# Moving part of the values' compression from a batch's end into the next batch, and its last product behind the dilated values

## The chip, the cores and the metric

The kernel runs on one core of a Trainium2 chip. The metric is the device time of one execution in microseconds. Its engines are PE (TensorE, matrix products; its weight loads are PEld), DVE (VectorE), ACT (ScalarE), POOL (GpSimd) and SP (SyncE, which here only issues DMAs). Each engine works its instructions off in program order; semaphores order them against each other.

## The reference

One inference step of a decoder with two layers, for a prompt of 512 rows and for eight sample sequences ("batches") of eight new rows with 2048 past positions. All is float32. Each layer norms and projects its rows, runs two groups of attention heads, and ends with an output projection and a squared-ReLU MLP. What matters here is the sparse group on the samples:

```python
# per batch: raw cached K/V rows -> 127 compressed tokens per K/V and head
parts.append(einsum('bncskd,scdh->bnskh', chunk + pe_half, w1[:, half]))   # 16 positions a chunk, 2 halves
hid = silu(sum(parts))
kvc = einsum('bnskh,shd->bnskd', hid, w2)          # s = 0 keys, s = 1 values
p_cmp = softmax(q . kvc_keys - alibi)
o_cmp = p_cmp . kvc_values
top   = 16 blocks of 64 rows by the summed p_cmp ("choice")
o_sel = attention over the chosen blocks (selection cache)
o_win = attention over the last 512 rows
```

The other group is an attention over dilated rows (distances 1, 4 and 16). The new rows' keys take part in each ("new scores").

## The kernel before

A layer is worked off in four stages: the projections (`project`), the prompt's attention in four rounds of twelve steps (`prompt_steps`), eight sample batches (`batch`, seven of them in a hardware loop with `more` true, the last one behind it), and 36 units of the output projection and the MLP (`unit`). The change touches the third and its two borders.

Nothing is scheduled by a planner: the order of each engine is the order of the text, and the same batch runs on all five engines at once. `Count.at(i, k)` is the value that a semaphore has after the k-th event of iteration i.

**PE in a batch**, `batch(it, more)` from L1357: the dilated scores of classes 0, 1 and 2 (L1371, 72 instructions in one row of a timeline), the new dilated rows (L1388); the second product of the compressed keys (L1395) and of the compressed values (L1401) from `hid`; the scores of the compressed, window and new keys (L1408 to L1413); the last dilated class (L1371 again), for which `kda` is loaded a second time by ACT (L758); importance sums and a transpose (L1421, L1425); the selection scores in two halves (L1431), of which the second goes into the bank that DVE reads importance from (L1994); transposes of the window's (L1441) and the dilated probabilities (L1449); the dilated values (L1463 to L1465, with one small product L1457 between); compressed and window values into bank 6 (L1470 to L1473); the transposes of the selection (L1480 to L1484); the selected values (L1496, L1500); the gathering of the outputs into bank 6 (L1508, L1513). Between the last of these stand the first products of the compression of the *next* batch, `compress(s, lo, hi, at)` (L1297): step j of 16 multiplies `w1[:, s, j]` with both heads' raw rows of residue j % 8 (two products, which the trace shows as four instructions); s is 0 for keys and 1 for values; the result gathers in a PSUM bank. After its last step, `h_full` is signalled. All 21 steps at the end of the batch are one group of 84 instructions in line L1303.

**The raw rows** lie in `raw`, one half of `ring` (2 MB), for one batch at a time. SP (from L524) reads the page numbers of batch b + 1 (L475), waits until both of batch b's hidden products are full (`h_full` at 2, L527), and only then issues nine of its sixteen raw pages; it waits for the dilated scores, issues the dilated keys (L496, L497), the other seven raw pages, waits for the window's and the dilated values' products, issues the window (L493) and the dilated values (L500), waits for the selected values' product and issues the sixteen selected pages (L478 stands for raw and selected pages alike). PE waits for all sixteen raw pages before the first key step of the next batch (L1487).

**The hidden layer** between the two products is made by ACT (`hidden_exp`, L744) and DVE (`hidden_batch`, L1930 to L1942: add one, reciprocal, multiply), one after the other for s = 0 and 1 at the end of a batch, through one buffer `he`. DVE then copies the compressed keys (L1971) and values (L1972), makes biased scores, the choice (L1993 to L2002), the minimum over the selection scores (L2017, L2020), and the outputs (L2026, L2033, L2054).

In a layer's first batch the raw rows were loaded beside the prompt, and `prompt_steps` holds 24 of the 32 steps of the compression at m = 12, 13 and 14, four ahead of and four behind the last products of the prompt (L1320 to L1335); L1520 has the other eight.

## Time and profile before

| | |
|---|---|
| median of three runs | 2443.39 us (2442.29 to 2445.78) |
| profiled execution | 2435.86 us, of which 2434.0 are its span |
| PE busy | 2291.6 us (94% of the span) |
| DVE, POOL, ACT busy | 904.7, 646.0, 553.0 us |
| mean share of the DMA engines, q1 | 47.0% |
| chain that ended last | PE 84%, DVE 5%, issue 5%, DMA 3%, ACT 2% |
| L1303 (compression) | 2048 instructions, 9% of the chain |

Busy time says which engine works, not what it waits for; the chain of waits says, backwards from the end, what each step was released by. A line L1303 is line 1303 of the kernel. In a timeline each row has a start, a duration, an engine, a line, the operand names and a count of merged instructions; brackets at its end are idle time ahead of it and who ended it. An averaged share hides that the stages differ: the sample batches run from about 384 to 709 us and from 1582 to 1905 us of the span.

### The profile page before, as it was taken

The numbers are of one execution on the slowest core, as the hardware profiler recorded it, in microseconds if no ns is written. First come the engines' busy times: TensorE is split into PE (matmuls) and PEld (weight loads), VectorE is DVE, ScalarE is ACT, GpSimd is POOL, SyncE is SP. The second block draws the span as 40 slices with busy tenths as digits, with TensorE's granted clock in tenths as the row PEclk, the third lists the DMA queues.
The fourth block names the chain that finished last, engine by engine and source line by source line (L and its number), as shares of the span: only waits on it lengthen the run. The fifth ranks groups of instructions, "written<-read, shape, count | busy, mean of one in ns | idle before, by whom it ended". The sixth has DMA issues, their size and how long they took to land.

```text
span 2434.0 us, 43176 instructions
## 1 busy us (share of the span) xinstructions
PE 2291.6 (94%) x13534; PEld 1610.0 (66%) x13534; DVE 904.7 (37%) x2423; ACT 553.0 (23%) x1306; POOL 646.0 (27%) x719
## 2 busy tenths in 40 slices
PE   7999888898899999999999998889899999999998
PEld 4544556667666777777745455667667667777776
DVE  2002663434344232336510146443433532223374
ACT  2101651111112422120211036411111133222202
POOL 0000771000132343434100037510010524343441
PEclk9999999999999999999999999999999999999999
DMA  9542016777863454445365220277777644454441
GB/s 342 197 166 74 23 53 242 247 284 261 298 238 149 165 209 175 176 162 200 122 259 190 104 86 0 79 280 289 257 287 259 241 159 163 163 211 173 178 161 40
DMA packets 128529, 448.19 MB, mean 184 GB/s; under 512 B 17921, under 2 KB 89474, under 8 KB 107266
## 3 DMA queue, kind: packets, MB, share of 16 engines
q1 hardware_dynamic: 118768, 416.45, 47.0%
q10 hardware_dynamic: 9618, 29.98, 3.6%
q8 instruction: 71, 1.16, 0.2%
q14 instruction: 72, 0.59, 0.1%
HBM read 435.76 MB, written 152.57 MB: 242 GB/s over the span
## 4 chain that ended last, share of the span: by engine, by line
PE 84%; DVE 5%; issue 5%; DMA 3%; ACT 2%; DVEq 1%; ACTq 0%; SPq 0%; POOLq 0%
PE bank L1036 37%; PE bank L1119 16%; PE bank L1303 9%; PE bank L1463 3%; DMA zone<-in_dilated_k 2%; PE bank L1250 2%; PE bank L1238 2%; PE bank L1371 2%; PE bank L1270 2%; PE bank L1496 1%; ACT zone L682 1%; PE bank L1017 1%; PE bank L1135 1%; PE bank L1465 1%; PE bank L1480 1%
## 5 line engine op out<-in xcount | busy, mean ns | idle before, releaser
L1036 PE MATMUL bank<-zone,ring 128*128 128x288 f32 x1664 | 425.8, 408 | 7.8 <-DVE zone L1637 5.2
L1119 PE MATMUL bank<-ring,hT 128*128 128x512 f32 (+3 forms) x960 | 396.4, 566 | 6.5 <-ACTq L727 5.0
L1036 PEld LDWEIGHTS bank<-zone,ring 128*128 128x128 f32 x1664 | 315.6, 190 | 101.3 <-DVE zone L1637 10.7
L1036 PE MATMUL bank<-zone,w 128*128 128x288 f32 x1408 | 353.6, 406 | 0.0
L1036 PEld LDWEIGHTS bank<-zone,w 128*128 128x128 f32 x1408 | 267.5, 190 | 73.9
L1119 PEld LDWEIGHTS bank<-ring,hT 128*128 128x128 f32 (+1 forms) x960 | 168.9, 181 | 197.3 <-issue 183.1
L1303 PE MATMUL bank<-ring,w 128*128 128x128 f32 x2048 | 242.4, 277 | 0.0
L845 POOL TENSOR_TENSOR w<-ring 128x512 f32<-128x512 f32 x72 | 94.8, 1317 | 553.3 <-PE bank L1036 312.3
L1303 PEld LDWEIGHTS bank<-ring,w 128*128 128x128 f32 x2048 | 233.1, 192 | 3.8 <-issue 3.8
L956 POOL TENSOR_TENSOR zone<-constants,stat 128x1024 f32<-128x1024 f32 x16 | 30.4, 1897 | 522.8 <-DVE stat L2002 522.8
L607 ACT COPY zone<-bank 128x288 f32<-128x288 f32 x72 | 28.7, 398 | 563.4 <-PE bank L1036 563.4
L1036 PE MATMUL bank<-xT,ring 128*128 128x288 f32 x512 | 136.0, 409 | 2.0 <-ACT zone L607 2.0
L682 ACT ACTIVATE zone<-zone,stat 128x128 f32<-128x128 f32 (+1 forms) x192 | 106.2, 554 | 102.9 <-DVE stat L1779 102.9
L1036 PEld LDWEIGHTS bank<-xT,ring 128*128 128x128 f32 x512 | 97.2, 191 | 29.6 <-ACT zone L607 2.9
L848 POOL TENSOR_TENSOR w<-w,ring 128x512 f32<-128x512 f32 x72 | 109.5, 1522 | 13.4 <-POOL w L845 13.4
L1779 DVE CUSTOM_DVE_ANT_0 zone<-bank,zone 128x128 f32<-128x128 f32 (+1 forms) x192 | 86.4, 488 | 71.7 <-PE bank L1238 63.9
L874 POOL COPY zone<-zone 128x128 f32<-128x128 f32 (+1 forms) x24 | 9.7, 403 | 361.5 <-ACT zone L654 361.5
L599 ACT ACTIVATE ring<-ring,gains 128x256 f32<-128x256 f32 x256 | 105.3, 494 | 0.0
L852 POOL TENSOR_TENSOR w<-ring,w 128x512 f32<-128x512 f32 x72 | 99.8, 1386 | 12.8 <-POOL ring L849 11.1
L1250 PE MATMUL bank<-c_ident,zone 128*128 128x128 f32 x480 | 75.6, 282 | 25.9 <-ACT zone L692 23.6
L1250 PEld LDWEIGHTS bank<-c_ident,zone 128*128 128x128 f32 x480 | 51.8, 142 | 69.9 <-issue 67.6
L654 ACT ACTIVATE zone<-bank,stat 128x512 f32<-128x512 f32 (+3 forms) x50 | 32.4, 648 | 284.8 <-PE bank L1119 284.8
(250 smaller groups left out, 2818.1 us busy)
## 6 DMA issues: line engine op xcount, KB each, us to landing
out_dil_s<-in_state_kv_dil SPq DMA_DIRECT2D x48, 2720.0 KB, 12.2
ring<-in_w_units SPq DMA_DIRECT2D x72, 1024.0 KB, 4.8
zone<-in_dilated_v SPq DMA_DIRECT2D x16, 3072.0 KB, 10.6
ring<-in_cache_kv_cmp SPq DMA_DIRECT2D x256, 128.0 KB, 2.6
ring<-in_cache_kv_sel SPq DMA_DIRECT2D x256, 128.0 KB, 5.7
ring<-in_w_in SPq DMA_DIRECT2D x10, 2048.0 KB, 8.0
zone<-in_dilated_k SPq DMA_DIRECT2D x16, 1280.0 KB, 5.9
zone<-in_dilated_k SPq DMA_DIRECT2D x16, 1024.0 KB, 7.8
```

Of the source, the lines that this page charges most:

```text
L599: last = nc.scalar.activation(w_[:, h, k], w_[:, h, k], ACT.Copy, scale=gain_of(l * 2 + 1, 4 * h + k))
L682: nc.scalar.activation(p_sb[:, slot, k, 0:w], p_sb[:, slot, k, 0:w], ACT.Exp, scale=-1.0, bias=stat[:, 16 + at:17 + at], accum_out=stat[:, ...
L845: nc.gpsimd.tensor_tensor(c_[:, 0], w_[:, 2], w_[:, 3], ALU.add).then_inc(s_comb.sem, 1)
L848: nc.gpsimd.tensor_tensor(c_[:, 1], c_[:, 0], w_[:, 0], ALU.subtract).then_inc(s_comb.sem, 1)
L852: nc.gpsimd.tensor_tensor(c_[:, 2], w_[:, 1], c_[:, 1], ALU.subtract).then_inc(s_comb.sem, 1)
L1036: last = mm(dst[:, 0:HALF], lhs[:, k, :], rhs(k), start=first and k == 0, stop=(k == 3), skip_group_check=True)
L1119: last = mm(dst, hT[:, k, t * P:t * P + ROWS[t]], ring[:, n % 2, k * CH:k * CH + width], start=start and k == 0, stop=stop and k == KT - 1)
L1238: last = mm(bank[2 * (m % 2) + k][:, 0:w], q[rows, t * P:(t + 1) * P], kT[rows, 0:w], start=True, stop=True)
L1250: last = tr(bank[4 + k][:, c * P:(c + 1) * P], p_sb[:, slot, k, c * P:(c + 1) * P], ident[:])
L1303: last = mm(out[:, k, first:first + P], w1[:, s, j, :], rawt[:, :, s, k, j % 8, :], start=(j == 0 and k == 0), stop=(j == 15 and k == 1), ...
L1463: mm(bank[7][32 * g:32 * g + M, :], ptd[:, e, at:at + M], vd[:, j, :], start=(j == 0), stop=False, skip_group_check=True)
L1779: V.tensor_tensor_reduce(p_sb[:, slot, k, 0:w], bank[2 * (m % 2) + k][:, 0:w], (p_bias if m < STEPS_A else p_biasd)[:, k, SEQ - w:SEQ], -1 ...
```

## The change

Of the values' 16 steps of compression, the first six (`V_AHEAD`) stay at the end of the batch in front; four (up to `V_NEW`) come behind the new scores and six (up to `V_CHOICE`) behind the choice's last transpose, both within the batch that uses them. They gather in bank 6 (`VHID_BANK`) in place of bank 5, behind a wait until DVE has taken the last outputs out of it. The second product of the values and DVE's copy of it move behind the dilated values, and the compressed values' product behind the window's. `hidden_exp` and `hidden_batch` are called once for the keys at the end of a batch and once for the values within it: on ACT behind the dilated probabilities, on DVE behind the minimum. In a layer's first batch, three and three value steps stand in the prompt's last step in place of four and four, and the eight behind it go. SP's program is not changed.

```diff
@@ -80,11 +80,12 @@
 TD_SD, TD_PTC, TD_PTW, TD_PTD, TD_PTS, TD_N = 0, 1, 2, 3, 4, 6
-SC_KTC, SC_VC, SC_S, SC_WIN, SC_NEW, SC_IMP, SC_SEL, SC_LEAST, SC_SUM, SC_OUT, SC_N = (
-    0, 1, 2, 3, 4, 5, 6, 8, 9, 10, 11)
+SC_KTC, SC_S, SC_WIN, SC_NEW, SC_IMP, SC_SEL, SC_LEAST, SC_VC, SC_SUM, SC_OUT, SC_N = (
+    0, 1, 2, 3, 4, 5, 7, 8, 9, 10, 11)
 SC_BANK = {SC_KTC: 2, SC_VC: 3, SC_S: 4, SC_WIN: 5, SC_NEW: 2, SC_IMP: 3, SC_SEL: 2, SC_SEL + 1: 3,
            SC_LEAST: 2, SC_SUM: 2, SC_OUT: 6}
-HID_BANK, FIRST_HID = (4, 5), (2, 3)
+HID_BANK, FIRST_HID, VHID_BANK = 4, 2, 6
+V_AHEAD, V_NEW, V_CHOICE, V_SEL = 6, 10, 16, 16
...
@@ -736,15 +737,15 @@
-                def hidden_exp(it, at):
-                    for s in range(2):
-                        act.wait_ge(h_full.sem, h_full.at(it, s + 1))
-                        act.wait_ge(h_done.sem, h_done.at(it, s))
-                        nc.scalar.activation(
-                            he.rearrange("p (k n) -> p k n", k=2),
-                            bank[at[s]][:, 0:258].rearrange("p (k n) -> p k n", k=2)[:, :, 1:129],
-                            ACT.Exp, scale=-1.0, bias=ncbias[:, s:s + 1]).then_inc(s_hexp.sem, 1)
+                def hidden_exp(it, s, at):
+                    act.wait_ge(h_full.sem, h_full.at(it, s + 1))
+                    act.wait_ge(h_done.sem, h_done.at(it, s))
+                    act.sem_inc(waits_taken_act, 1)
+                    nc.scalar.activation(
+                        he.rearrange("p (k n) -> p k n", k=2),
+                        bank[at][:, 0:258].rearrange("p (k n) -> p k n", k=2)[:, :, 1:129],
+                        ACT.Exp, scale=-1.0, bias=ncbias[:, s:s + 1]).then_inc(s_hexp.sem, 1)
@@ -763,6 +764,7 @@
                     probs(s_d, 3, slice(0, P))
+                    hidden_exp(it, 1, VHID_BANK)
                     act.wait_ge(td_full.sem, td_full.at(it, TD_PTW + 1))
...
-                hidden_exp(l * NB, FIRST_HID)
+                hidden_exp(l * NB, 0, FIRST_HID)
                 with act.Fori(0, NB - 1) as b:
                     batch(b)
-                    hidden_exp(l * NB + b + 1, HID_BANK)
+                    hidden_exp(l * NB + b + 1, 0, HID_BANK)
                 batch(NB - 1)
@@ -1318,21 +1320,23 @@
-                        compress(0, 0, 4, FIRST_HID[0])
+                        compress(0, 0, 4, FIRST_HID)
...
                     if ends and m == STEPS + 2:
-                        compress(1, 0, 4, FIRST_HID[1])
+                        pe.wait_ge(og_a.sem, og_a.at(l, ROUNDS))
+                        pe.sem_inc(waits_taken_pe, 1)
+                        compress(1, 0, V_AHEAD // 2, VHID_BANK)
...
                     if ends and m == STEPS + 2:
-                        compress(1, 4, 8, FIRST_HID[1])
+                        compress(1, V_AHEAD // 2, V_AHEAD, VHID_BANK)
@@ -1395,12 +1399,6 @@
-                    pe.wait_ge(h_done.sem, h_done.at(it, 2))
-                    B = bank[SC_BANK[SC_VC]]
-                    for k in range(2):
-                        last = mm(B[:, k * HD:(k + 1) * HD], hid[:, 1, k * P:(k + 1) * P], w2[:, 1, :],
-                                  start=(k == 0), stop=(k == 1), skip_group_check=True)
-                    last.then_inc(sc_full.sem, 1)
@@ -1412,6 +1410,7 @@
                     mm(B[low, 64:128], q_a, kns[:], start=True, stop=True, skip_group_check=True).then_inc(
                         sc_full.sem, 1)
+                    compress(1, V_AHEAD, V_NEW, VHID_BANK)
                     pe.wait_ge(kda_ld.sem, kda_ld.at(it, 2))
                     dilated_class(ND_A + 4).then_inc(td_full.sem, 1)
@@ -1423,6 +1422,7 @@
                     tr(bank[TD_PTC % 2][:, 0:64], s_c, ident[0:64, 0:64]).then_inc(td_full.sem, 1)
+                    compress(1, V_NEW, V_CHOICE, VHID_BANK)
                     pe.wait_ge(sel_ld.sem, sel_ld.at(it, NPG))
@@ -1465,13 +1465,20 @@
-                    pe.wait_ge(sc_used.sem, sc_used.at(it, 0))
+                    pe.wait_ge(sc_used.sem, sc_used.at(it, SC_LEAST + 1))
+                    pe.wait_ge(h_done.sem, h_done.at(it, 2))
+                    B = bank[SC_BANK[SC_VC]]
+                    for k in range(2):
+                        last = mm(B[:, k * HD:(k + 1) * HD], hid[:, 1, k * P:(k + 1) * P], w2[:, 1, :],
+                                  start=(k == 0), stop=(k == 1), skip_group_check=True)
+                    last.then_inc(sc_full.sem, 1)
                     O = bank[6][:, 0:P]
-                    mm(O[low], ptc, vc, start=True, stop=True, skip_group_check=True)
                     for c in range(4):
                         mm(O[high], ptw[:, c, :], kw_sb[:, c, 128:256], start=(c == 0), stop=False, skip_group_check=True)
-                    mm(O[high], ptw[0:64, 4, :], vsm[:, 128:256], start=False, stop=True,
-                        skip_group_check=True).then_inc(win_pv.sem, 1)
+                    mm(O[high], ptw[0:64, 4, :], vsm[:, 128:256], start=False, stop=True, skip_group_check=True)
+                    pe.wait_ge(sc_used.sem, sc_used.at(it, SC_VC + 1))
+                    pe.sem_inc(waits_taken_pe, 1)
+                    mm(O[low], ptc, vc, start=True, stop=True, skip_group_check=True).then_inc(win_pv.sem, 1)
...
@@ -1514,10 +1521,11 @@
                     if more:
-                        compress(0, 11, 16, HID_BANK[0])
-                        compress(1, 0, 16, HID_BANK[1])
-                compress(1, 8, 16, FIRST_HID[1])
+                        compress(0, 11, 16, HID_BANK)
+                        pe.wait_ge(sc_used.sem, sc_used.at(it, SC_OUT + 1))
+                        pe.sem_inc(waits_taken_pe, 1)
+                        compress(1, 0, V_AHEAD, VHID_BANK)
@@ -1927,20 +1935,20 @@
-                def hidden_batch(it, at):
-                    horder = Order(ch_h, it)
-                    for s in range(2):
-                        dve.wait_ge(s_hexp.sem, s_hexp.at(it, s + 1))
-                        V.tensor_scalar(he, he, 1.0, None, ALU.add).then_inc(horder.sem, 1)
-                        dve.wait_ge(horder.sem, horder.next())
-                        V.reciprocal(he, he).then_inc(horder.sem, 1)
-                        dve.wait_ge(horder.sem, horder.next())
-                        V.scalar_tensor_tensor(
-                            hid[:, s, :].rearrange("p (k n) -> p k n", k=2),
-                            bank[at[s]][:, 0:258].rearrange("p (k n) -> p k n", k=2)[:, :, 1:129], cbias[:, s:s + 1],
-                            he.rearrange("p (k n) -> p k n", k=2), ALU.add, ALU.mult).then_inc(h_done.sem, 1)
-                    if horder.k != 4:
+                def hidden_batch(it, s, at):
+                    horder = Order(ch_h, it, 2 * s)
+                    dve.wait_ge(s_hexp.sem, s_hexp.at(it, s + 1))
+                    dve.sem_inc(waits_taken_dve, 1)
+                    V.tensor_scalar(he, he, 1.0, None, ALU.add).then_inc(horder.sem, 1)
+                    dve.wait_ge(horder.sem, horder.next())
+                    V.reciprocal(he, he).then_inc(horder.sem, 1)
+                    dve.wait_ge(horder.sem, horder.next())
+                    V.scalar_tensor_tensor(
+                        hid[:, s, :].rearrange("p (k n) -> p k n", k=2),
+                        bank[at][:, 0:258].rearrange("p (k n) -> p k n", k=2)[:, :, 1:129], cbias[:, s:s + 1],
+                        he.rearrange("p (k n) -> p k n", k=2), ALU.add, ALU.mult).then_inc(h_done.sem, 1)
+                    if horder.k != 2:
                         raise ValueError(horder.k)
...
@@ -1969,7 +1977,6 @@
                     V.tensor_copy(ktc, small(SC_KTC)[:, 0:P]).then_inc(sc_used.sem, 1)
-                    V.tensor_copy(vc, small(SC_VC)[:, 0:P]).then_inc(sc_used.sem, 1)
                     negated(s_c, small(SC_S)[low, 0:P], const["b_cmp"][:], stat[low, 24:25]).then_inc(sc_used.sem, 1)
@@ -2020,6 +2027,7 @@
                     V.tensor_tensor(stat[:, 27:28], small(SC_LEAST)[:, 0:1], sm[:, 19:20], ALU.min).then_inc(sc_used.sem, 1)
                     dve.wait_ge(sc_used.sem, sc_used.at(it, SC_LEAST + 1))
                     dve.sem_inc(s_max.sem, 1)
+                    hidden_batch(it, 1, VHID_BANK)
...
+                    V.tensor_copy(vc, small(SC_VC)[:, 0:P]).then_inc(sc_used.sem, 1)
                     dve.wait_ge(od_full.sem, od_full.at(it, 1))
...
-                hidden_batch(l * NB, FIRST_HID)
+                hidden_batch(l * NB, 0, FIRST_HID)
                 with dve.Fori(0, NB - 1) as b:
                     batch(b)
-                    hidden_batch(l * NB + b + 1, HID_BANK)
+                    hidden_batch(l * NB + b + 1, 0, HID_BANK)
                 batch(NB - 1)
```

## Rows read from the trace of the kernel before

**Rows 1.** Chain that ended last, whole span: start, duration, engine, line, count.

```profile
455.19 1.90 PE bank L1496 x32
...
498.98 1.90 PE bank L1496 x32
...
540.12 1.90 PE bank L1496 x32
...
705.73 1.94 PE bank L1496 x32
...
1878.14 2.78 PE bank L1371 x72
...
1900.94 1.94 PE bank L1496 x32
```

**Rows 2.** Timeline of PE, one batch of layer 0: start, duration; idle before in brackets.

```profile
547.24 9.62 PE L1303 MATMUL bank<-ring,w 128*128 128x128 f32 x84
556.70 2.94 PE L1371 MATMUL bank<-zone 128*128 128x128 f32 x72
...
560.98 0.66 PE L1401 MATMUL bank<-w,zone 128*128 128x64 f32 x4
561.56 0.32 PE L1408 MATMUL bank<-zone,q_s 128*64 128x128 f32 x1
...
563.96 1.08 PE L1371 MATMUL bank<-zone 128*32 128x128 f32 x32 [1.20 <-DMA zone<-in_dilated_k]
...
567.59 1.08 PE L1431 MATMUL bank<-ring,q_s 128*64 128x512 f32 x4 [1.07 <-DVE topk L1994]
...
570.07 0.66 PE L1449 MATMUL bank<-c_ident,zone 128*128 128x128 f32 x4 [0.95 <-DVE zone L2006]
571.53 2.08 PE L1463 MATMUL bank<-zone 128*128 128x512 f32 x10 [0.81 <-ACT zone L773]
...
578.23 1.09 PE L1480 MATMUL bank<-c_ident,zone 128*128 128x128 f32 x8
...
579.67 1.58 PE L1303 MATMUL bank<-ring,w 128*128 128x128 f32 x12
```

**Rows 3.** Timeline of SP's queue, the same batch.

```profile
561.61 5.30 SPq L478 DMA_DIRECT2D ring<-in_cache_kv_cmp  x9
...
568.33 3.92 SPq L478 DMA_DIRECT2D ring<-in_cache_kv_cmp  x7
...
583.68 7.77 SPq L478 DMA_DIRECT2D ring<-in_cache_kv_sel  x16
```

**Rows 4.** Timeline of PE, the start of each layer's first batch.

```profile
384.46 2.17 PE L1371 MATMUL bank<-zone 128*128 128x128 f32 x40 [2.84 <-DMA zone<-in_dilated_k]
...
1582.34 1.84 PE L1371 MATMUL bank<-zone 128*128 128x128 f32 x28 [2.73 <-DMA zone<-in_dilated_k]
```

**Rows 5.** Timeline of DVE, the batch of rows 2.

```profile
550.67 1.75 DVE L1937 RECIPROCAL zone<-zone 128x256 f32<-128x256 f32 x1
...
574.18 0.16 DVE L2020 TENSOR_TENSOR stat<-bank,sm 128x1 f32<-128x1 f32 x1 [0.47 <-PE bank L1457]
```

**Rows 6.** Line L475 on SP, from 590 to 603 us.

```profile
L475 SPq TENSOR_LOAD <-pages x16: 262/263/276, 592.0 to 601.7; - x16
```

**Rows 7.** DMA issues, 561 to 562.3 and 571.8 to 572.3: median us to landing last.

```profile
ring<-in_cache_kv_cmp SPq DMA_DIRECT2D x2, 128.0 KB, 2.5
...
ring<-in_cache_kv_cmp SPq DMA_DIRECT2D x1, 128.0 KB, 6.3
```

**Rows 8.** Timeline of PE, a gap among the units of layer 0.

```profile
768.48 2.95 PE L1036 MATMUL bank<-hT,w 128*128 128x288 f32 x6 [2.38 <-DVE zone L1696]
```

**Rows 9.** Stretches: engines' busy us (instructions), mean granted clock, DMA share, GB/s.

```profile
766.00:774.00 8.00, 5.62 (x17) 3.98 (x16) 4.86 (x9) 0.30 (x1) 1.10 (x1) 0.79 0.08 14
1580.00:1588.00 8.00, 5.34 (x91) 4.45 (x93) 3.35 (x6) 0.47 (x1) 0.00 (x0) 1.00 1.00 389
```

**Rows 10.** Timeline of SP's queue, the last batch of layer 0.

```profile
687.51 0.33 SPq L552 DMA_DIRECT2D ring<-in_w_units  x1
```

More of the change, by code:

```diff
@@ L1320, in prompt_steps @@
                         pe.sem_inc(waits_taken_pe, 1)
-                        compress(0, 0, 4, FIRST_HID[0])
+                        compress(0, 0, 4, FIRST_HID)
                     if ends and m == STEPS + 1:
-                        compress(0, 8, 12, FIRST_HID[0])
+                        compress(0, 8, 12, FIRST_HID)
                     if ends and m == STEPS + 2:
-                        compress(1, 0, 4, FIRST_HID[1])
+                        pe.wait_ge(og_a.sem, og_a.at(l, ROUNDS))
+                        pe.sem_inc(waits_taken_pe, 1)
+                        compress(1, 0, V_AHEAD // 2, VHID_BANK)
                     if m == 9:
@@ L1330, in prompt_steps @@
                     if ends and m == STEPS:
-                        compress(0, 4, 8, FIRST_HID[0])
+                        compress(0, 4, 8, FIRST_HID)
                     if ends and m == STEPS + 1:
-                        compress(0, 12, 16, FIRST_HID[0])
+                        compress(0, 12, 16, FIRST_HID)
                     if ends and m == STEPS + 2:
-                        compress(1, 4, 8, FIRST_HID[1])
+                        compress(1, V_AHEAD // 2, V_AHEAD, VHID_BANK)
                     if m == 10:
@@ L1487, in batch @@
                         pe.wait_ge(raw_ld.sem, raw_ld.at(it + 1, NPG))
-                        compress(0, 0, 3, HID_BANK[0])
+                        compress(0, 0, 3, HID_BANK)
                     O = bank[3][:, 0:P]
@@ L1502, in batch @@
                     if more:
-                        compress(0, 3, 11, HID_BANK[0])
+                        compress(0, 3, 11, HID_BANK)
                     B = bank[SC_BANK[SC_OUT]]
```

## The prediction

> **What bounds the kernel now.** I read first the chain of work that ended last, over the whole span: in the sample batches it is nearly all TensorE (PE), interrupted at the same few places in each. The lines L1496 in it mark one place of each batch [rows 1]: 498.98 to 540.12 is a batch of 41.14 us, 455.19 to 498.98 one of 43.79. Then the timeline of PE in one batch of 41.14 us [rows 2]. The brackets show where it idles: 1.20 us before L1371's last class (a load of `kda`), 1.07 in L1431 (VectorE, top-k), 0.95 before L1449 (VectorE), 0.81 before L1463 (ScalarE's copies). The sum is 4.03 us, of which the change can fill the first three, 3.22 us. Everything else in the batch is PE at work, so PE's order is the bound, as long as loads and VectorE keep up. Last the queue of SP [rows 3], because the change moves the last product of the compression, and SP waits for that product before it overwrites `raw`.
>
> The changed stretch runs from the first L1371 of a layer's batches [rows 4] to the last L1496 [rows 1]: 705.73 - 384.46 = 321.3 us in layer 0, 1900.94 - 1582.34 = 318.6 us in layer 1, together 639.9 us in which 14 batches go through the loop.
>
> **PE's work, part by part.** I count in us from the batch's first L1371 (556.70).
> - At the end of the batch ten sixteenths of the values' compression go. 84 instructions take 9.46 us from start to start of the next group (547.24 to 556.70 [rows 2]), 0.1126 us each; ten steps are 40 instructions, -4.50 us.
> - Four of them (16 instructions, 1.80 us) come after the new scores, where PE goes idle at 562.76 = 6.06. They end at 7.86. ScalarE's load ends at about 7.2 (PE goes on at 563.96 = 7.26), so the wait of 1.20 us is filled and 0.60 us is added.
> - Six (24 instructions, 2.70 us) come after the choice's last transpose. Between 563.96 and the first L1431, at 567.59 - 1.07 - 1.08 = 565.44, lie 1.48 us, so these products run from 9.34 to 12.04. VectorE, which is about 0.2 us later than now, has released the second L1431 by 567.59 + 0.2 = 11.1 and the transposes of L1449 by 570.07 + 0.2 = 13.6; PE reaches them at 13.1 and 14.6. Both waits (1.07 and 0.95) go. The 0.81 us before L1463 stays, because it is ScalarE's answer to L1449 itself. So L1463 comes 4.50 - 3.22 = 1.28 us later.
> - L1401 (0.58 us from start to start, 560.98 to 561.56) leaves its place and gains nothing there: VectorE's copy of `ktc` has to end before L1408 anyway, and L1401 was its cover. At its new place it adds 0.58 us.
> - At its new place it also waits for the second `hidden_batch`, which VectorE starts after L2020. L2020 now runs at 574.18 = 17.48 and moves 1.24 us, to 18.7. The reciprocal of 1.75 us [rows 5] with its two neighbours is about 2.7 us, so it is done at 21.6; PE is there at 20.15 + 1.28 = 21.4. I take 0.2 us. VectorE's copy of `vc` lies beside the window's products, which now stand between L1401 and L1470.
> - L1480 therefore starts at 578.23 - 556.70 = 21.53 + 1.28 + 0.58 + 0.20 = 23.6, which is 2.06 later.
> - The wait for VectorE's last copy ahead of the new bank 6 products costs nothing: five steps of key compression (2.3 us) cover a copy that starts about 0.3 us after L1513. If that cover were gone it would cost 0.5 us.
> Were that all, a batch would take 41.14 + 2.06 - 4.50 = 38.70 us.
>
> **The queue of SP.** At the loop's top SP reads page numbers, waits until both hidden products are full, issues nine raw pages, two loads of dilated keys and seven raw pages. The 16 numbers are read from 592.0 to 602 [rows 6], after the last selected page (583.68 + 7.77 = 591.5 [rows 3]); that is 4.5 after the next batch's start (597.8), and raw loading starts at 561.61 = 4.91 [rows 3]. The wait is long satisfied now, since the products end at 556.70. In the changed kernel SP sends the selected pages 2 to 6 us later and has the numbers by about 9.4, but the values are full at 12.04. So the wait decides, and raw loading starts at 12.2, more than 7 us later, while its reader (L1303 at 579.67 = 22.97) moves by only 2.06 to 25.03. Queued behind this wait on SP are the dilated keys, the window, the dilated values and the next selected pages.
> How long does the load take? The first raw issue is at 561.61, the last at 568.33 + 3.92 - 0.33 = 571.92, and it lands 6.3 us later [rows 3, 7]: 16.6 us from first issue to last landing. The last seven land so late because 2.3 MB of dilated keys stand in front of them; the first two pages land in 2.5 us [rows 7]. Nothing in the change shortens this. So the last page lands at 12.2 + 16.6 = 28.8, and PE waits 28.8 - 25.0 = 3.8 us before its first key products of the next batch. That wait also swallows the 0.2 us for `hidden_batch`. A batch is then 28.8 + (41.14 - 22.97) - 4.50 = 42.47 us, 1.33 more than a fast batch now. The later loads have room: selected pages are read 12 us into the next batch, dilated values 16 us into it.
>
> **The clock.** In the trace a PE gap of 2.38 us [rows 8] was followed by 3.4 us at a granted clock of 0.5, that is 1.2 GHz (8 us with a mean of 0.79, against 1.00 in the other window [rows 9]), which costs 1.7 us of work. A gap of 2.73 us was followed by none [rows 4, 9]. The slow batches of now (six of 14 are longer by 2.4 to 2.65 us) are of this kind: after the three gaps, L1463 runs at half clock. The change fills those gaps, but makes one of 3.8 us, longer than any of these, and it stands in front of dense products. I take a drop in four batches of five, 1.7 us each: 1.36 per batch, so 43.83 us. The bounds are 0 and 2.65 us, a whole slow batch of now.
> On this the Trainium skill ("TensorE: Matmul & The Clock Gate", section "HAM oscillation") describes a kernel that waits for a load in each tile and starts every tile at half clock. By that rule all 14 would pay, an estimate of 5 us more than mine; the rows, with one gap of two followed by a drop, let me stay below it.
>
> **A layer's first batch.** The keys' load waits for a copy of the prompt's last products, and in the prompt's last step but one now three and three steps of compression stand ahead of them, not four and four: two steps, -0.9 us. The eight steps before the first L1371 go out of a stretch where PE waited for this load anyway, so nothing else is gained; the gap of 2.84 us [rows 4] grows by 32 instructions of 0.12 us to about 6.7 us and I charge a drop, +1.7.
> **The last batch** has no raw page to wait for: from its first L1371 to L1496 22.80 us [rows 1], plus 2.06, is 24.86. There SP's first weight load (687.51 [rows 10]) moves back about 5 us to the end of the values; its reader on PE comes only after L1496 and the output products, more than 20 us behind, and POOL's combinations run beside. I price it at nothing; at most 5 us per layer if that cover is gone.
>
> **The sum.** Per layer -0.9 + 1.7 + 7 x 43.83 + 24.86 = 332.5, two layers 664.9 us, against 639.9: +25. The profiled execution took 2435.9 us (span 2434.0), 7.5 below the median of the runs, 2443.4. Three more half-clock stretches would explain that difference, and such stretches are removed by the change. So I add not 25 but 21 to the median: 2464 us. About 0.2% (5 us) is what a measurement can tell from no change.
>
> **The rivals.**
> - Raw pages in time, a faster kernel. Mechanism: the filled gaps count in full since the load fits between 12.0 and 25.0. For it speaks that single pages land in 2.5 us. Against it speaks that issuing alone takes 10.3 us, and then 6.3 to land. Price: 14 x 38.70 + 51.3 = 593.1, -47 us, 2396 us. It decides below a batch of (639.9 - 51.3) / 14 = 42.04 us, a wait of 3.3 us with no clock loss: the load would have to be 0.5 us shorter to break even and 3.8 us shorter for all of it. Chance 0.12.
> - The wait comes, but the clock stays up: 14 x 42.47 + 51.3 = 645.9, +6, 2449 us; with the lead of the median gone, half of this is no change. Chance 0.17.
> - The clock falls for two stretches in each batch, 45.1 us: 683, +43, 2486 us. Chance 0.09.
> - My forecast, wait and usual clock loss: 0.62.
> The range leaves out the first and part of the third: 2443 to 2482. Slower by over 0.2%: 0.62 + 0.09 + half of 0.17 = 0.79; within: 0.08; faster: 0.13.
>
> **What would show it.** In the trace after: the brackets before L1371, the second L1431 and L1449 gone; L1401 at its new place behind a wait under 0.5 us; SP's first raw page about 12 us after the batch's L1371, directly behind the last value product; PE's largest wait at L1303, for a DMA of `cache_kv_cmp`, 3 to 4 us in 14 batches; the granted clock at 0.5 right behind it in most. Wrong if that wait is under 3 us, if the raw pages start before 9, or if PE waits longer for `hidden_batch` than for the pages.

## The result and the profile after

The changed kernel takes 2483.97 us (median of four runs, 2479.11 to 2484.28) against 2442.84 us before (four runs, 2438.03 to 2445.78). The ratio is 1.0166, with a 95% interval of 1.0145 to 1.0186: 41 us slower, where 21 were forecast and the range ended at 2482. The profiled execution took 2484.28 us, of which 2482.5 are its span.

The page of the changed kernel, the engines' busy time and the shares of the chain that ended last:

```profile
PE 2322.6 (94%) x13534; PEld 1647.2 (66%) x13534; DVE 902.8 (36%) x2423; ACT 553.0 (22%) x1306; POOL 645.6 (26%) x719
...
PE 80%; issue 5%; SPq 5%; DMA 4%; DVE 4%; ACT 1%; DVEq 0%; ACTq 0%; POOLq 0%
PE bank L1038 36%; PE bank L1121 16%; PE bank L1305 10%; SPq L479 4%; DMA ring<-in_cache_kv_cmp 4%; PE bank L1375 3%; PE bank L1252 2%; PE bank L1240 2%; PE bank L1503 2%; PE bank L1272 2%; ACT zone L683 1%; PE bank L1019 1%; PE bank L1137 1%; PE bank L1392 1%; PE bank L1515 1%
```

PE issues as many instructions as before, and its share of the chain falls from 84 to 80%. New in the chain are the raw pages: SP's issues of them (L479) and their landing, 4% each. (Most lines move by two to seven: L1303 is now L1305, L1371 is L1375, L1408 is L1406, L1480 is L1487, L1496 is L1503. The two products that change their place are L1401, now L1472, and L1470, now L1481.)

PE's waits by line and releaser, total us, times, longest:

```profile
PE bank L1305 <- DMA ring<-in_cache_kv_cmp: 45.9, 14, 3.6
...
PE bank L1375 <- DMA zone<-in_dilated_k: 13.1, 2, 6.6
...
PE bank L1472 <- DVE zone L1947: 9.5, 16, 1.6
```

The 14 batches of the loop each wait for the raw pages, 3.3 us on average. The waits before the second L1431 and before L1449 are gone. The one for `kda` is left in the two first batches, where it is the long gap. The batch that answers to [rows 2] on PE:

```profile
571.59 2.94 PE L1375 MATMUL bank<-zone 128*128 128x128 f32 x72
...
576.43 0.32 PE L1406 MATMUL bank<-zone,q_s 128*64 128x128 f32 x1 [0.50 <-DVE zone L1979]
...
577.56 2.05 PE L1305 MATMUL bank<-ring,w 128*128 128x128 f32 x16
579.54 1.08 PE L1375 MATMUL bank<-zone 128*32 128x128 f32 x32
...
581.02 2.94 PE L1305 MATMUL bank<-ring,w 128*128 128x128 f32 x24
583.90 1.94 PE L1431 MATMUL bank<-ring,q_s 128*64 128x512 f32 x8
...
587.59 2.11 PE L1463 MATMUL bank<-zone 128*128 128x512 f32 x10 [0.72 <-ACT zone L775]
...
593.42 0.63 PE L1472 MATMUL bank<-w,zone 128*128 128x64 f32 x4 [0.52 <-DVE zone L1947]
...
600.89 2.39 PE L1305 MATMUL bank<-ring,w 128*128 128x128 f32 x12 [3.59 <-DMA ring<-in_cache_kv_cmp]
```

The ten steps stand where the waits were, and L1463 comes at 16.0 us from the batch's start, as worked out (16.1). Then the gap of 3.59 us. SP's queue in this batch, to be laid beside [rows 3], and the landings beside [rows 7] (issues from 579 to 585 and from 591 to 592.5, the median to landing last):

```profile
584.25 4.87 SPq L479 DMA_DIRECT2D ring<-in_cache_kv_cmp  x9
589.46 0.33 SPq L497 DMA_DIRECT2D zone<-in_dilated_k  x1
589.98 0.33 SPq L498 DMA_DIRECT2D zone<-in_dilated_k  x1
590.54 4.29 SPq L479 DMA_DIRECT2D ring<-in_cache_kv_cmp  x7
```

```profile
ring<-in_cache_kv_cmp SPq DMA_DIRECT2D x2, 128.0 KB, 2.0
...
ring<-in_cache_kv_cmp SPq DMA_DIRECT2D x2, 128.0 KB, 6.8
```

The first raw page is issued at 584.25 = 12.66 us into the batch, 0.3 us after the last value product; before it was 4.9. PE may go on 600.89 - 584.25 = 16.6 us later, the load's length before.

The clock behind the gap (a stretch's length, busy us of PE, PEld, DVE, ACT, POOL, mean granted clock, DMA share, GB/s):

```profile
418.00:430.00 12.00, 8.89 (x74) 7.73 (x73) 1.84 (x6) 0.58 (x1) 0.00 (x0) 0.86 1.05 424
```

A mean of 0.86 over 12 us is 3.4 us at 0.5 (1.2 GHz). All 14 gaps are followed by such a stretch. In the two first batches the clock also fell inside the gap of 6.5 us before L1375, for 6.8 us, of which 3.6 to 4.7 lie behind the gap.

Where the 41 us lie is best seen by stage, from the first L1371 (L1375) of a layer's batches to the last L1496 (L1503), and from one batch's start to the next, both from timelines of PE. The experiments below are in the same table.

| kernel | layer 0 | layer 1 | sum | shortest and longest of 14 batches | the two last batches |
|---|---|---|---|---|---|
| before | 321.2 | 318.6 | 639.8 | 41.1, 43.8 | 25.6, 22.9 |
| after | 342.6 | 337.3 | 679.9 | 43.9, 46.5 | 29.8, 25.7 |
| e1_all_ahead | 333.0 | 333.7 | 666.7 | 42.6, 48.2 | 25.8, 25.8 |
| e2_raw_first | 311.8 | 314.5 | 626.3 | 39.8, 41.2 | 30.2, 31.9 |
| e3_before_raw_first | 321.4 | 318.6 | 640.0 | 41.1, 43.8 | 22.9, 22.9 |
| e4_busy_gap | 330.2 | 328.4 | 658.6 | 42.4, 44.7 | 29.2, 28.3 |
| e5_gate_early | 327.5 | 327.5 | 655.0 | 41.3, 44.6 | 30.4, 30.3 |
| e6_pool_later | 337.6 | 338.6 | 676.2 | 44.1, 46.6 | 25.7, 25.7 |
| e7_tuned | 304.6 | 307.0 | 611.6 | 39.5, 40.4 | 26.7, 28.8 |
| e8_tuned_late | 304.4 | 305.2 | 609.6 | 39.2, 40.7 | 26.4, 27.0 |

679.9 - 639.8 = 40.1 us, and the medians differ by 41.1, so nearly the whole loss lies in the sample batches. (The two profiled executions differ by 48.4 us. The start of the program accounts for most of the other 8, see below.) Where a time of an experiment is compared with the changed kernel's, it goes by what each lost or won against the kernel before in its own series, whose median was 2442.84 for the changed kernel, 2438.66 for e1 to e4, 2439.69 for e5 to e7 and 2441.7 for e8.

### The profile page after: what moved, and what is told of

The parts are those of the page before. It is cut to its first block, busy times and chain, and to the rows that moved or that the text cites. A ratio compares the mean times of both kernels' runs of the same rounds, so it can differ in the third digit from the quotient of the medians.

```text
span 2482.5 us, 43270 instructions
## 1 busy us (share of the span) xinstructions
PE 2322.6 (94%) x13534; PEld 1647.2 (66%) x13534; DVE 902.8 (36%) x2423; ACT 553.0 (22%) x1306; POOL 645.6 (26%) x719
## 4 chain that ended last, share of the span: by engine, by line
PE 80%; issue 5%; SPq 5%; DMA 4%; DVE 4%; ACT 1%; DVEq 0%; ACTq 0%; POOLq 0%
PE bank L1038 36%; PE bank L1121 16%; PE bank L1305 10%; SPq L479 4%; DMA ring<-in_cache_kv_cmp 4%; PE bank L1375 3%; PE bank L1252 2%; PE bank L1240 2%; PE bank L1503 2%; PE bank L1272 2%; ACT zone L683 1%; PE bank L1019 1%; PE bank L1137 1%; PE bank L1392 1%; PE bank L1515 1%
## 5 line engine op out<-in xcount | busy, mean ns | idle before, releaser
L1121 PE MATMUL bank<-ring,hT 128*128 128x512 f32 (+3 forms) x960 | 400.4, 571 | 6.0 <-ACTq L728 4.9
L1305 PE MATMUL bank<-ring,w 128*128 128x128 f32 x2048 | 262.3, 287 | 45.9 <-DMA ring<-in_cache_kv_cmp 45.9
L1121 PEld LDWEIGHTS bank<-ring,hT 128*128 128x128 f32 (+1 forms) x960 | 170.4, 183 | 199.4 <-issue 185.3
L1305 PEld LDWEIGHTS bank<-ring,w 128*128 128x128 f32 x2048 | 245.5, 198 | 53.4 <-DMA ring<-in_cache_kv_cmp 47.1
L958 POOL TENSOR_TENSOR zone<-constants,stat 128x1024 f32<-128x1024 f32 x16 | 30.3, 1897 | 561.1 <-DVE stat L2009 561.1
L756 ACT ACTIVATE zone<-zone,stat 64x128 f32<-64x128 f32 (+1 forms) x64 | 48.7, 760 | 237.1 <-DVE stat L1967 133.7
L1252 PE MATMUL bank<-c_ident,zone 128*128 128x128 f32 x480 | 76.7, 285 | 25.8 <-ACT zone L693 23.5
```

What stands on the lines that cost most here:

```text
L1121: last = mm(dst, hT[:, k, t * P:t * P + ROWS[t]], ring[:, n % 2, k * CH:k * CH + width], start=start and k == 0, stop=stop and k == KT - 1)
L1252: last = tr(bank[4 + k][:, c * P:(c + 1) * P], p_sb[:, slot, k, c * P:(c + 1) * P], ident[:])
L1305: last = mm(out[:, k, first:first + P], w1[:, s, j, :], rawt[:, :, s, k, j % 8, :], start=(j == 0 and k == 0), stop=(j == 15 and k == 1), ...
```

## The experiments

**The place of the ten steps alone.** e1_all_ahead undoes only the move of the steps:

```diff
-V_AHEAD, V_NEW, V_CHOICE, V_SEL = 6, 10, 16, 16
+V_AHEAD, V_NEW, V_CHOICE, V_SEL = 16, 16, 16, 16
...
+                compress(1, 8, 16, VHID_BANK)
                 with pe.Fori(0, NB - 1) as b:
```

> The changed kernel with all 16 steps of the values' compression back at the end of the batch in front (V_AHEAD = V_NEW = V_CHOICE = 16), all else of the change kept. Theory (the wait of SP for the full values makes the raw pages late): the pages start 5 us into a batch again, the 3.0 to 3.6 us wait of PE in front of the next key steps is gone, the three gaps of before are back, and a batch costs about 1.1 us more than before (the moved second product 0.58, its wait 0.5): about 2460 us. Rival (the moved product, the new bank and the split of the hidden layer cost the time): it stays near 2484 us.

Measured: 2467.3 us against 2438.66 in the same runs, ratio 1.0125 (1.0097 to 1.0154), +29. No wait for raw pages is left, and the gaps are back. In its timelines of SP and PE, for the batch that starts at 567.32:

```profile
572.23 5.31 SPq L479 DMA_DIRECT2D ring<-in_cache_kv_cmp  x9
```

```profile
574.64 1.75 PE L1375 MATMUL bank<-zone 128*32 128x128 f32 x32 [1.28 <-DMA zone<-in_dilated_k]
...
581.18 0.66 PE L1449 MATMUL bank<-c_ident,zone 128*128 128x128 f32 x4 [0.95 <-DVE zone L2014]
582.56 2.11 PE L1463 MATMUL bank<-zone 128*128 128x512 f32 x10 [0.72 <-ACT zone L775]
588.56 0.63 PE L1472 MATMUL bank<-w,zone 128*128 128x64 f32 x4 [0.53 <-DVE zone L1948]
```

Raw pages start 4.9 us into the batch again. So the late pages hang on the place of the last value product. But the theory's price for the rest was low: the rest of the change costs 27 of the 40 us of the stage. A batch without half clock takes 42.63 us in place of 41.14, 1.5 more where 1.1 were worked out. The missing 0.4 us is in the product of the compressed values. Its two passes in the kernel before, and in the changed kernel (timelines of PE):

```profile
576.85 0.32 PE L1470 MATMUL bank<-zone 128*64 128x128 f32 x1
576.86 0.32 PE L1472 MATMUL bank<-zone 128*64 128x128 f32 x1
577.01 0.27 PE L1470 MATMUL bank<-zone 128*64 128x128 f32 x1
577.02 0.93 PE L1472 MATMUL bank<-zone 128*64 128x128 f32 x7
```

```profile
595.36 0.43 PE L1481 MATMUL bank<-zone 128*64 128x128 f32 x2
595.72 1.09 PE L1487 MATMUL bank<-c_ident,zone 128*128 128x128 f32 x8
```

Before, each pass of L1470 (64 columns of the array, `O[low]`) started 0.01 us beside one of the window's (L1472, `O[high]`, the other 64). Behind the window's products it stands alone and takes 0.36 us from start to start. Over 14 batches 1.5 us are 21 us of the 27; 3 us are in the last batches, the rest in more half clock.

**The order of SP's loads.** e2_raw_first changes SP alone, and e3_before_raw_first makes the same edit in the kernel before:

```diff
-                    load_raw(page, range(0, 9))
+                    load_raw(page, range(0, NPG))
                     sp.wait_ge(td_full.sem, td_full.at(it, TD_SD + 1))
                     load_dilated_k(b + 1)
-                    load_raw(page, range(9, NPG))
```

> The changed kernel, but SP issues all 16 raw pages before the two loads of dilated keys. Theory (the last seven pages are late because 2.3 MB of keys stand in front of them): the first page starts 12.7 us into the batch, the last is issued at about 21.7 and lands about 2.3 us later at 24.0, before PE asks at 25.7. No wait, no half clock behind it, a batch of about 39.4 us in place of 44.5: 14 x 5.1 = 71 us less, 2413 us. Rival (the loads as a whole do not fit in a shorter batch, so the wait moves to the keys, the dilated values or the selected pages): between 2450 and 2484 us, with a wait of PE for another load.

> The kernel before with the same order of SP's loads. Theory: there the raw pages have 1.5 us to spare and the keys 10 or more, so nothing waits for either; 2443 us, within 0.2%. Rival (the order is better or worse for the DMA engines in itself): a difference of more than 5 us.

Measured: e2 2428.48 us, ratio 0.9964 (0.9944 to 0.9984) to before; e3 2440.11 us, ratio 1.0009 (0.9993 to 1.0026). In e2 the wait for raw pages is gone; its timelines of SP and PE, its landing of the last pages, its longest wait in the batches, and the flight of ScalarE's load of `kda`, in e2 and in the kernel before:

```profile
639.90 8.83 SPq L479 DMA_DIRECT2D ring<-in_cache_kv_cmp  x16
```

```profile
635.18 1.08 PE L1374 MATMUL bank<-zone 128*32 128x128 f32 x32 [0.51 <-DMA zone<-in_dilated_k]
```

```profile
ring<-in_cache_kv_cmp SPq DMA_DIRECT2D x2, 128.0 KB, 2.3
```

```profile
PE bank L1374 <- DMA zone<-in_dilated_k: 27.2, 16, 6.5
```

```profile
zone<-in_dilated_k ACTq DMA_DIRECT2D x1, 1024.0 KB, 6.1
```

```profile
zone<-in_dilated_k ACTq DMA_DIRECT2D x1, 1024.0 KB, 4.9
```

The batch starts at 626.65; pages are issued from 13.3 to 22.1 and the last lands 2.3 us after its issue, at 24.1, while PE asks at 652.81 = 26.2. The gate is no earlier than in the changed kernel, only the 2.3 MB of keys no longer stand in front of seven pages, and that is worth 679.9 - 626.3 = 54 us of the stage. The same order gives nothing to the kernel before, where no page was late.

The forecast of 2413 was 15 us too low. A batch takes 39.34 us and the wait for ScalarE's load of `kda` on top of it: the shortest, 39.81 us, has a wait of 0.47, the longest, 41.21 us, one of 1.87. In the 12 later loop batches this wait is 0.9 us on average (0.5 in the batch shown), in the last batches it is 1.8 and 2.0 us, and the last batches take 30 and 32 us for one reason more (see e6). The traces say why the load is late. Wherever the last selected page had landed before ScalarE issued its load, 2.3 us into the batch, the load took 4.7 to 5.3 us, 84 of 84 times in six runs. In e2 SP sends the selected pages later, the last of them lands 6.0 to 6.7 us into the batch in 11 of the 12 later loop batches, and `kda` lands 2.5 us behind it in each of the 11. No run moves the selected pages alone, so this is a close tie between two landings and not an experiment.

**The clock.** e4_busy_gap fills the gap with products that nobody reads:

```diff
+                        for n in range(13):
+                            mm(bank[5][:, 0:P], ident[:], const["all_ones"][:], start=True, stop=True)
                         pe.wait_ge(raw_ld.sem, raw_ld.at(it + 1, NPG))
```

> The changed kernel with 13 products of constants (26 instructions, about 3.1 us) into the free bank 5 just ahead of PE's wait for the raw pages; nothing reads them. The wait's end is set by the load and stays. Theory (each gap is followed by 3.4 us at half clock, 1.7 us of work lost): the half-clock stretches behind the gap vanish, 14 x 1.7 = 24 us less, 2460 us. Rival (the half clock is not caused by the gap, or costs nothing since loads set the pace): 2484 us or more.

Measured: 2458.87 us, ratio 1.0096 (1.0058 to 1.0134) to before. That is +20 us where the changed kernel had +41, so 21 us less, and the stage says the same (658.6 against 679.9). Its timeline of PE, and the stretch that answers to the one at 418 above:

```profile
625.81 3.15 PE L1495 MATMUL bank<-c_all_ones,c_ident 128*128 128x128 f32 x26
629.31 1.60 PE L1305 MATMUL bank<-ring,w 128*128 128x128 f32 x12 [0.35 <-DMA ring<-in_cache_kv_cmp]
```

```profile
411.00:423.00 12.00, 11.47 (x113) 10.59 (x111) 1.54 (x6) 0.58 (x1) 0.00 (x0) 1.00 1.02 410
```

The load ends when it did, PE's products start when they did, and they run at full clock: 12 instructions in 1.60 us in place of 2.39. None of the 14 is followed by a half-clock stretch any more. So the gap costs twice, about 3.3 us of waiting and 1.7 us of half clock behind it, each time. This is the rule of the Trainium skill ("TensorE: Matmul & The Clock Gate", section "HAM oscillation"): a kernel that waits for a load in each tile starts every tile cold. The trace agrees, 14 of 14. The prediction had named the rule and counted four drops of five.

**The gate's time.** e5_gate_early puts all ten steps behind the new scores:

```diff
-V_AHEAD, V_NEW, V_CHOICE, V_SEL = 6, 10, 16, 16
+V_AHEAD, V_NEW, V_CHOICE, V_SEL = 6, 16, 16, 16
```

> The changed kernel with all ten in-batch steps behind the new scores (V_NEW = 16), none behind the choice. The values are full about 1.4 us earlier in the batch (about 10.9 in place of 12.3 us), but PE's order is worse: the waits for VectorE before the second L1431 and before L1449 (1.07 and 0.95 us) come back. Theory (a batch lasts as long as gate, load and tail together): it becomes shorter by the 1.4 us in spite of the two waits, 14 x 1.4 = 20 us less, 2464 us, and the wait in front of the key steps shrinks to about 1 us. Rival (PE's own order still sets the batch): the waits add, 2484 us plus up to 28.

Measured: 2454.03 us, ratio 1.0071 (1.005 to 1.0092) to before: +14 where the changed kernel had +41, 27 us less, of which the stage shows 25. Its longest waits of PE, and its timeline of SP in the batch that starts at 556.07:

```profile
PE bank L1449 <- DVE zone L2013: 15.2, 16, 1.0
PE bank L1431 <- DVE topk L2001: 14.7, 16, 1.1
```

```profile
567.06 4.87 SPq L479 DMA_DIRECT2D ring<-in_cache_kv_cmp  x9
```

PE's order is worse by two waits of 1 us, and yet the batch is shorter, 41.34 us where no half clock falls into it (six of the 14) against 44.3, and 42.1 on average over the later loop batches: raw pages start at 11.0 in place of 12.7, and PE asks for them 1.9 us later, at 583.71 = 27.6. Together they close the gap altogether (none is left, 1 us was expected), and with it goes the half clock behind it. The half clock of the kernel before comes back with the two waits, in the other batches. Here the two waits themselves cost nothing that the load would not have taken.

**The last batch of a layer.** e6_pool_later holds back GpSimd's first combination of weights:

```diff
                 pool.wait_ge(h_full.sem, h_full.at(l * NB + NB - 1, 2))
+                pool.wait_ge(h_done.sem, h_done.at(l * NB + NB - 1, 2))
```

> The changed kernel, but GpSimd starts to combine weights in a layer's last batch only when VectorE's second hidden_batch is done. Theory (the two run on each other's time): VectorE's TENSOR_SCALAR there takes 0.29 us again and not 1.40, PE's wait for it 0.5 us and not 1.6, and the 10 us at half clock behind it in layer 0 shrink; 1 to 5 us less in all, 2480 us. Rival (the long operation has another cause): it stays at 1.4 us in layer 0.

Measured: 2482.19 us, ratio 1.0171 (1.0143 to 1.0199) to before; this can't be told from the changed kernel. The stage shows it. VectorE's `hidden_batch` in layer 0's last batch in the changed kernel, with what GpSimd does then, and the same operation with GpSimd held back:

```profile
723.97 1.40 DVE L1943 TENSOR_SCALAR zone<-zone 128x256 f32<-128x256 f32 x1 [0.35 <-DVE stat L2027]
```

```profile
723.93 1.28 POOL L850 TENSOR_TENSOR w<-w,ring 128x512 f32<-128x512 f32 x1 [0.18 <-POOL w L847]
```

```profile
723.64 0.30 DVE L1944 TENSOR_SCALAR zone<-zone 128x256 f32<-128x256 f32 x1 [0.35 <-DVE stat L2028]
```

The operation takes 1.40 us beside a GpSimd TENSOR_TENSOR of nearly the same span and 0.30 us without it. ScalarE's long ACTIVATE runs beside it in both, so it is not the cause. By all cases on record it hangs on which of the two starts first. GpSimd was first by 0.04 us here, and by 0.01 to 0.09 us in both layers of e2 and e4, where the operation took 1.35 to 1.42 us. In layer 1 of the changed kernel VectorE was first by 0.02 us, and it was not held up:

```profile
1942.33 0.29 DVE L1943 TENSOR_SCALAR zone<-zone 128x256 f32<-128x256 f32 x1 [0.35 <-DVE stat L2027]
1942.35 1.41 POOL L850 TENSOR_TENSOR w<-w,ring 128x512 f32<-128x512 f32 x1 [0.18 <-POOL w L847]
```

The trace of the kernel before had shown this already. The same operation waits there for the end of a GpSimd MEMSET ahead of each layer's batches, where it cost PE nothing:

```profile
378.72 1.40 POOL L960 MEMSET zone<- 128x1560 f32 x1 [12.53 <-ACT hT L698]
...
378.98 1.29 DVE L1935 TENSOR_SCALAR zone<-zone 128x256 f32<-128x256 f32 x1 [5.99 <-ACT zone L744]
```

PE's wait for it in e6 falls from 1.62 to 0.52 us, the half clock behind it goes, and the last batch takes 25.7 us in place of 29.8. At the end of the batch 1.1 us of it come back as a longer wait of the first unit.

**A kernel that beats both.** e7_tuned has the order of e2 and the hold of e6, and three edits more:

```diff
-V_AHEAD, V_NEW, V_CHOICE, V_SEL = 6, 10, 16, 16
+V_AHEAD, V_COPY, V_NEW, V_CHOICE = 6, 7, 12, 16
...
+                    compress(1, V_AHEAD, V_COPY, VHID_BANK)
                     q_a = q_s[:]
...
-                    compress(1, V_AHEAD, V_NEW, VHID_BANK)
+                    compress(1, V_COPY, V_NEW, VHID_BANK)
...
-                        if j == ND_A:
+                        if j == 3:
                             pe.wait_ge(s_least.sem, s_least.at(it, 1))
...
+                for n in range(26):
+                    mm(bank[5][:, 0:P], ident[:], const["all_ones"][:], start=True, stop=True)
                 with pe.Fori(0, NB - 1) as b:
```

> All raw pages ahead of the dilated keys and GpSimd later, as in the two runs with one of these alone, and three more edits: one of the four steps behind the new scores moves in front of them (it covers VectorE's copy of the keys, 0.50 us), two more steps come behind them in its place (they cover the 0.5 us wait for ScalarE's load of keys), the small product L1457 comes behind three tiles of dilated values and not five (VectorE's hidden_batch 0.8 us earlier, the wait of 0.53 us gone), and 26 products of constants stand in a layer's first gap. If each wait is worth its length: a batch of about 38.4 us against 39.9 with the raw pages first alone, 14 x 1.5 = 21 us, plus 3 to 8 us from the clock: about 2402 us. If something else then ends last, it stays near 2428 us.

Measured: 2414.05 us, ratio 0.9913 (0.9887 to 0.9939) to before. A batch takes 39.5 us and not 38.4. The waits for the keys' copy and for `hidden_batch` are gone, but the small product now waits inside the dilated values:

```profile
598.54 2.09 PE L1464 MATMUL bank<-zone 128*128 128x512 f32 x6 [0.72 <-ACT zone L774]
600.75 0.38 PE L1458 MATMUL bank<-sm,constants 128*128 128x1 f32 x2
```

Six instructions take 2.09 us where ten take 2.11 elsewhere. e8_tuned_late sets `j == 3` back to `j == ND_A`:

> The tuned kernel, but the small product L1457 back behind five tiles of dilated values. Behind three tiles PE stood 0.8 us inside the dilated values, since VectorE has the selection's minimum only 17.9 us into the batch, and lost 1.0 us where 0.53 was to be won. Theory (VectorE's chain from the choice to the minimum is what ends last now): PE comes there just when the minimum is ready, and waits at most 0.4 us for hidden_batch: 39.1 us a batch in place of 39.5, 5 us less, 2409 us. Rival (the place of the product makes no difference): 2414 us.

Measured: 2413.12 us, ratio 0.9885 (0.9868 to 0.9902) to before; by these times the two can't be told apart, as the rival said. Its timeline of PE:

```profile
598.28 2.11 PE L1464 MATMUL bank<-zone 128*128 128x512 f32 x10 [0.72 <-ACT zone L774]
600.49 0.38 PE L1458 MATMUL bank<-sm,constants 128*128 128x1 f32 x2
...
604.28 0.63 PE L1473 MATMUL bank<-w,zone 128*128 128x64 f32 x4 [0.52 <-DVE zone L1950]
```

The small product comes at the same point of the batch in both, 17.9 us after the batch's start, when VectorE has the minimum. Where PE doesn't wait inside the values, it waits behind them for `hidden_batch`, which VectorE starts from the same minimum. So PE can't win more than a little here by its own order. The little is there, though. Batches without a wait for `kda` take 39.2 us in e8 and 39.46 in e7, as the theory had it (39.1). The gain goes in longer waits for `kda`, 5.2 us in the 12 later loop batches against 1.6 in e7. The rival had the time right for another reason than its own.

## Why the prediction was wrong, and where it was right

**Right: the mechanism and its place.** The queue of SP step holds in each of its parts. The gate decides and not the page numbers: SP's first page is 12.7 us into the batch (12.2 worked out), the load takes 16.6 us (16.6), PE waits for `cache_kv_cmp` at the key steps in all 14 loop batches, 2.9 to 3.6 us (3.8). e1 and e2 show both causes, the late gate and the keys in front of the last pages; either undone removes the wait. PE's work part by part holds too: three waits filled, L1463 at 16.0, L1401 without gain where it was, since L1406 now waits 0.50 us for the copy that L1401 covered. The wait for the dilated keys before a layer's first L1371 grew to 6.5 us (6.7). L1487 starts at 24.1 and not 23.6: the wait for `hidden_batch` is 0.5 us (0.2 worked out), and the step missed that L1470 ran beside the window's products and now takes 0.36 us of its own. Up to the wait for the pages this lies in front of a load that ends later anyway, so it costs nothing in the loop here; in e1 and in the last batches it does.

**Wrong: the size, +21 for +41.** The steps that failed are terms of the sum. For the stage, the first L1371 to the last L1496 of both layers, the prediction's terms give 2 x (1.7 + 7 x 43.83 + 24.86) - 639.9 = +26.8 us; it measured +40.1. Three terms make up the 13.3 us between them, and two more lie outside the stage.
- The clock and the load: four batches of five at 1.7 us were taken, and it was 14 of 14 at about 1.7, as e4 shows. PE also goes on at 29.0 us on average and not at 28.8. This makes the later loop batches 44.34 us on average in place of 43.83: 6 us over twelve of them.
- The last batches, the largest mistake in kind: priced at 24.9 us each, they took 29.8 and 25.7, together 5.7 us more. Of this, 4.1 is the weight combination of GpSimd. The step said that POOL's combinations "run beside" and priced them at nothing. They were beside PE, but on VectorE's time, and VectorE has a new operation there which PE waits for. The range had no case for it. That it came in one layer only was luck, decided by 0.02 to 0.04 us. The other 1.6 us are L1470 alone, the longer wait for `hidden_batch` and small change.
- The first batches: 46.5 and 46.0 us in place of 45.5, 1.4 us.
- The 0.9 us per layer for two steps fewer ahead of the first L1371 lie in front of the stage. The traces hardly show them: that L1371 starts at 384.02 to 384.89 us in e2, e4 and e5, against 384.46 and 385.34 in the kernel before and e3, five programs that started at the same clock.
- The base: the sum gave +25 against the profiled execution, and 4 us were taken off for the median, on the ground that the slower runs had more half-clock stretches in their batches. With the plain sum the forecast would have been 2468 us. Nothing on record shows that ground. The slower of 33 runs of the kernel before (2432 to 2447 us) do have the lower mean clock (0.989 to 0.981), but where their stretches lie no trace shows, and the two traces at hand differ elsewhere, at the start of the program.

The 26 us from 17 us on, in the kernel before and after, with the mean granted clock third from the end:

```profile
17.00:43.00 26.00, 22.04 (x72) 11.93 (x73) 5.16 (x10) 5.72 (x10) 1.17 (x1) 0.87 1.05 399
```

```profile
17.00:43.00 26.00, 21.10 (x60) 11.16 (x59) 5.36 (x11) 6.14 (x11) 1.17 (x1) 0.67 1.05 412
```

The profiled execution of before had 6.8 us at half clock at the program's start and the one of after 17.1. At the same product group of the projections they are 5.5 us apart (L1121 at 237.15 us against L1119 at 231.62), long before any changed instruction, and the one of after had another half-clock stretch of 6.8 us at 250 us; at the first L1371 they are 7.5 us apart. That is about what lies between the profiled time (2435.86) and the median (2442.84) of before. So the start can explain that difference alone, and the change can't remove it; that it does explain it stays open.

**The rivals.** Raw pages in time (0.12) did not come about, and e2 shows what it would have given: 2428 and not 2396. A batch of 38.7 us was worked out; 39.34 is what PE's order gives (most of the difference is the longer wait for `hidden_batch` and L1470, as above), 0.9 is the wait for ScalarE's load, and the last batches cost 12 us more than worked out. The clock stays up (0.17) is e4, 2459 where 2449 was worked out. Two stretches in each batch (0.09, 2486 us) has the measured time and the wrong reason: behind the raw pages' gap each batch had one stretch of 3.4 us.

What stays open: whether ScalarE's keys in e2 are late only because of the selected pages, since no run moves these alone, and what made the unprofiled runs of before slower than the profiled one.

## What to carry to other kernels

When a product moves later, look for the DMA queue that waits for it: the filled waits were worth 3.2 us a batch, and the seven us by which the reload of its input started later cost more, until the order of the queue was put right. Order a queue by when each load's reader comes, not by when its buffer is free: sixteen pages in front of two loads of keys made the same change 54 us better in its stage and turned it from 1.7% slower to 0.4% faster. A gap on PE that recurs costs more than its length when the clock falls behind it, and "beside" has to be asked of each engine: an operation of GpSimd that costs PE nothing can still hold up the VectorE operation that PE waits for. Look in the trace of before for the operation that is to move: here it stood there thirty times with 0.29 us and twice with 1.29, and the two long ones had GpSimd beside them.

## What the runs showed of the hardware

- A VectorE TENSOR_SCALAR of 128x256 float32 in SBUF took 0.29 to 0.30 us alone. It took 1.35 to 1.42 us when a GpSimd TENSOR_TENSOR of 128x512 (1.28 us) had started 0.01 to 0.09 us ahead of it (five of five), 1.15 to 1.29 us behind a GpSimd MEMSET, and 0.29 us when it started 0.02 us ahead of the TENSOR_TENSOR, which then took 1.41 us (one case). The reciprocal and the multiply behind it kept their 1.75 and 0.48 us beside the same kind of operation.
- Gaps of 2.9 to 3.9 us ahead of dense products were followed by 3.4 us at 1.2 GHz in 28 of 28 cases (the changed kernel and e6). The length alone doesn't decide below that: the gap of 2.4 us that each layer has among its units was followed by such a stretch in 13 of 20 cases over the ten runs, and the gap of 2.7 to 2.8 us before a layer's first batch in one of six (the kernel before, e1, e3).
- A 128 KB page lands 2.0 to 2.5 us after its issue on a free queue, and 6.3 to 6.8 us after it behind 2.3 MB on the same queue.
- ScalarE's load of 1 MB took 4.7 to 5.3 us when SP's sixteen selected pages had landed before it was issued, and 6.1 to 7.7 us in e2, where they had not.
